# Reordering the Hyena transforms of a two-block transformer kernel: wide products on VectorE, GpSimd without arithmetic there, tables loaded early, gate projections between the steps

## The reference, cut to what matters

```python
def long_conv_bidir(u, h_fwd, h_bwd, bias):
    k2 = jnp.concatenate([h_fwd, jnp.zeros((1, C)), h_bwd[:0:-1]], axis=0)
    U = jnp.fft.rfft(u, n=2 * L, axis=1)
    K = jnp.fft.rfft(k2, n=2 * L, axis=0)
    y = jnp.fft.irfft(U * K[None], n=2 * L, axis=1)[:, :L]
    return y + u * bias

def hyena_mixer(hv, hx1, hx2, ...):
    z, gates = parts[0], parts[1:]          # after a short convolution
    for n in range(2):
        z = gates[n] * long_conv_bidir(z, filt[:, 0, n], filt[:, 1, n], bias[n])
    return z

m = sigmoid(g_na) * (y_na @ w_na_o) + sigmoid(g_hy) * (y_hy @ w_hy_o)
x = x + g1 * (m @ w_out)                    # then the feed-forward part, then a norm
```

## Time and profile before

| | us |
|---|---|
| median of three runs | 1063.85 |
| lowest, highest | 1062.31, 1063.89 |
| profiled execution, device time | 1062.26 |
| its span in the profile | 1060.4 |
| PE busy | 997.3 (94%) |
| DVE (VectorE) busy | 830.4 (78%) |
| ACT (ScalarE) busy | 566.2 (53%) |
| POOL (GpSimd) busy | 166.7 (16%) |

### The profile page before, as it was taken

One profiled execution on the slowest core, in us unless ns is written; L12 is line 12 of the kernel. 1 busy time (PEld: TensorE's weight loads), 2 busy tenths in 40 slices (PEclk: granted clock), 3 DMA queues, 4 the chain that ended last, 5 costly groups with the idle time before them and its releaser, 6 DMA issues.

```text
span 1060.4 us, 19534 instructions
## 1 busy us (share of the span) xinstructions
PE 997.3 (94%) x7946; PEld 964.0 (91%) x7946; DVE 830.4 (78%) x1360; ACT 566.2 (53%) x1062; POOL 166.7 (16%) x172
## 2 busy tenths in 40 slices
PE   7798999999899999999999999998798999999996
PEld 7798999999898879999999988988798899999996
DVE  7799999686898876899977678888888667776453
ACT  7544444435676655555555535665354456665442
POOL 5113222101000003001201110221632210000001
PEclk9899999999999999999999999999999999999998
DMA  9546466665434323788856613331334435645441
GB/s 289 210 162 227 168 240 210 228 226 212 174 124 153 127 100 135 275 335 304 289 213 238 224 53 143 120 135 60 160 120 159 160 131 189 214 184 192 167 159 40
DMA packets 33721, 192.19 MB, mean 181 GB/s; under 512 B 4912, under 2 KB 6256, under 8 KB 14816
## 3 DMA queue, kind: packets, MB, share of 16 engines
q1 hardware_dynamic: 23520, 157.46, 40.7%
q10 hardware_dynamic: 6912, 25.17, 7.0%
q0 software_dynamic: 3200, 8.32, 2.5%
HBM read 187.78 MB, written 3.15 MB: 180 GB/s over the span
## 4 chain that ended last, share of the span: by engine, by line
PE 66%; DVE 21%; ACT 6%; issue 3%; DMA 2%; POOL 1%; DVEq 0%; SPq 0%; ACTq 0%
PE ps L93 64%; DVE wl L70 7%; ACT wh L67 3%; DVE ab L70 3%; DMA raw<-w 2%; PE ps L96 1%; DVE junk L84 1%; DVE s L77 1%; DVE fh L70 1%; ACT s L67 1%; POOL wl L70 1%; DVE hl L70 1%; DMA cst<-cst 1%; DVE s L84 0%; DVE x L73 0%
## 5 line engine op out<-in xcount | busy, mean ns | idle before, releaser
L70 DVE TENSOR_TENSOR wl<-raw,wh 128x1024 fp32r<-128x1024 f32 x276 | 340.4, 1248 | 39.1 <-ACT wh L67 38.8
L67 ACT ACTIVATE wh<-raw 128x1024 fp32r<-128x1024 f32 x286 | 294.9, 1049 | 8.1 <-DMA raw<-w 3.4
L93 PE MATMUL ps<-xh,wh 128*128 128x256 f32 (+1 forms) x992 | 280.6, 283 | 5.9 <-ACT sghy L67 2.5
L93 PE MATMUL ps<-xh,wl 128*128 128x256 f32 (+1 forms) x992 | 278.3, 281 | 0.0
L93 PE MATMUL ps<-xl,wh 128*128 128x256 f32 x992 | 278.1, 280 | 0.0
L93 PE MATMUL ps<-xt,wh 128*128 128x272 f32 (+1 forms) x1120 | 224.9, 295 | 12.7 <-DVE fg L70 5.9
L93 PEld LDWEIGHTS ps<-xt,wh 128*128 128x128 f32 x1120 | 181.9, 193 | 17.6 <-DVE fg L70 7.0
L93 PEld LDWEIGHTS ps<-xh,wh 128*128 128x128 f32 x992 | 188.6, 190 | 7.1 <-ACT sghy L67 2.7
L93 PEld LDWEIGHTS ps<-xh,wl 128*128 128x128 f32 x992 | 189.1, 191 | 0.2
L93 PEld LDWEIGHTS ps<-xl,wh 128*128 128x128 f32 x992 | 188.7, 190 | 0.0
L93 PE MATMUL ps<-xt,wl 128*128 128x272 f32 (+1 forms) x560 | 162.5, 290 | 0.0
(11 more groups left out here) (333 smaller groups left out, 1665.2 us busy)
## 6 DMA issues: line engine op xcount, KB each, us to landing
raw<-w SPq DMA_DIRECT2D x141, 1024.0 KB, 4.9
ada<-ada ACTq DMA_DIRECT2D x37, 512.0 KB, 4.4
cb<-ada ACTq DMA_DIRECT2D x11, 512.0 KB, 3.4
raw<-w SPq DMA_DIRECT2D x4, 512.0 KB, 6.4
spare<-w SPq DMA_DIRECT2D x2, 1024.0 KB, 9.5
spectra<-ev POOLq DMA_DIRECT2D x8, 256.0 KB, 3.6
ks<-spectra POOLq DMA_DIRECT2D x2, 1024.0 KB, 6.2
skew<-rpb POOLq DMA_DIRECT2D x8, 192.0 KB, 3.2
```

Of the source, the lines that this page charges most:

```text
L67: return Issued(self.e and self.e.activation(out, src, func, **kw))
L70: return Issued(self.e and self.e.tensor_tensor(out, a, b, op))
L93: return Issued(self.e and self.e.matmul(out, stat, mov, start=start, stop=stop))
```

## The change

The transforms are written anew around the same arithmetic.

1. `fwd_dve`, `fwd_pool` and `fwd_end_dve` become `fwd_split`, `fwd_products`, `fwd_sums` and `fwd_low`, all on VectorE. The four products of a half are two instructions of 128x1024 in place of four of 128x512, two of which were GpSimd's.
2. GpSimd makes no low parts of gate halves any more. It issues DMAs, and does no arithmetic between the last score bias and the sums `m` of the merge (six of the eight, VectorE does the last two).
3. The table F is loaded before the attention and split there; G and half of the first spectrum (`ksh`) are loaded before the attention ends.
4. The transforms (0,0) and (0,1) begin inside the attention's last steps. The other steps stand at new places between the gates. All forward transforms use banks 3 and 4, all inverse ones 5 and 6, all transposes 7.
5. Slot 5 comes back into the ring for the fourth half of the output projection and no longer for its first.

```diff
     def on_pool(self, h):
-        g = self.W.half_of(("gate", 0))
-        return h < 3 or (g <= h < g + 16 and (h - g) % 3 == 2)
+        return h < 3
...
             if h == last:
-                order.insert(0, 5)
+                order.insert(3, 5)
...
     (second_pe)
-        self.na_turn(P, 3, 1, 0), self.na_turn(P, 3, 1, 1)
+        self.na_turn(P, 3, 1, 0)
+        self.fwd_pe(P, 0, 0)
+        self.na_turn(P, 3, 1, 1)
         self.gate_pe(P, 1)
+        self.fwd_pe(P, 0, 1)
         self.na_av(P, 7)
...
+    def fwd_products(self, V, n, half):
+        a, b = [self.pair(t) for t in self.fwd_bufs(n, half)]
+        k = self.spectrum(n, half)
...
+        V.tt(b, a, k, ALU.mult).then_inc(S["hy_v"], ("v1", n, half))
+        V.wait_ge(S["hy_v"], ("v1", n, half))
+        V.tt(a, a, k[:, :, ::-1, :], ALU.mult).then_inc(S["hy_v"], ("v2", n, half))
+    def fwd_sums(self, V, n, half):
...
+        V.tt(b[:, :, 0, :], b[:, :, 0, :], b[:, :, 1, :], ALU.subtract).then_inc(S["hy_v"], ("y1", n, half))
+        V.wait_ge(S["hy_v"], ("v2", n, half))
+        V.wait_ge(S["hy_v"], ("y1", n, half))
+        V.tt(b[:, :, 1, :], a[:, :, 0, :], a[:, :, 1, :], ALU.add).then_inc(S["hy_v"], ("y2", n, half))
+        V.wait_ge(S["hy_v"], ("y2", n, half))
+        V.tt(at[:, :512], bt[:, :512], bt[:, 512:], ALU.add).then_inc(S["hy_v"], ("w", n, half, 0))
+        V.tt(at[:, 512:], bt[:, :512], bt[:, 512:], ALU.subtract).then_inc(S["hy_v"], ("w", n, half, 1))
...
     def tail_pe(self, P):
-        gate(2)
-        self.fwd_pe(P, 0, 0)
-        gate(3)
-        self.fwd_pe(P, 0, 1)
-        gate(4, 5, 6)
+        gate(2, 3, 4)
         self.inv_pe(P, 0, 0)
-        gate(7, 8)
+        gate(5, 6)
+        self.inv_pe(P, 0, 1)
+        gate(7)
         self.fwd_pe(P, 1, 0)
-        self.inv_pe(P, 0, 1)
-        gate(9, 10)
+        gate(8)
         self.fwd_pe(P, 1, 1)
-        gate(11)
+        gate(9, 10, 11)
         self.inv_pe(P, 1, 0)
         gate(12)
         self.hy_back(P, 0)
-        gate(13, 14, 15)
-        self.nao_pe(P, 0), self.nao_pe(P, 1)
+        gate(13, 14)
         self.inv_pe(P, 1, 1)
-        self.nao_pe(P, 2), self.nao_pe(P, 3)
+        gate(15)
         self.hy_back(P, 1)
-        for d in range(4, 8):
+        for d in range(8):
             self.nao_pe(P, d)
...
     (second_pool: early loads)
+        for m in (0, 1):
+            G.dma(self.ksh[:, 512 * m:512 * (m + 1)]..., self.kd[0, ...]).then_inc(S["ld_ksh"], ...)
+        G.dma(self.dftg[:, :], self.ins["dft1"][:, 512:1024]).then_inc(S["ld_dftg"], ("load",), by=16)
```

More of the change, by code:

```diff
@@ L417, in cast, with casts @@
         A.act(self.wh[s][:, :], src, ACT.Copy).then_inc(self.S["w_hi"], use)
-    def casts(self, A, spent):
+    def casts(self, A, spent, most=None):
         W = self.W
-        while A.next_half < W.halves:
+        end = W.halves if most is None else min(W.halves, A.next_half + most)
+        while A.next_half < end:
             b = W.before[("half", A.next_half)]
@@ L440, in rests @@
         V.spent = max(V.spent, spent)
-        while V.next_half < W.halves:
+        end = W.halves if most is None else min(W.halves, V.next_half + most)
+        while V.next_half < end:
             b = W.before[("half", V.next_half)]
@@ L2071, in second_act @@
             ath(2 * p, 0), ath(2 * p, 1)
-            soft(4 * p + 3)
+            if p < 3:
+                soft(4 * p + 3)
         self.z_hi(A, 0, 0), self.z_hi(A, 0, 1)
+        soft(15)
         self.gate_act(A, 0)
         oh(6)
+        self.fwd_act(A, 0, 0)
+        A.wait_ge(S["ld_dftg"], ("load",))
+        A.wait_ge(S["na_v"], ("min", 15))
+        A.act(self.GH[:, :], self.dftg[:, :], ACT.Copy).then_inc(S["hy_a"], ("tab", 1))
         ath(7, 0), ath(7, 1)
         self.gate_act(A, 1)
+        self.fwd_act(A, 0, 1)
         oh(7)
@@ L2261, in second_pool @@
                     S[f"ld_skew{hd % 2}"], ("head", hd + 2), by=16)
+        for m in (0, 1):
+            G.wait_ge(S[f"st_kd{m}"], ("kd", 1, 1))
+        G.wait_ge(S["na_v"], ("min", 14))
+        for m in (0, 1):
+            G.dma(self.ksh[:, 512 * m:512 * (m + 1)].rearrange("p (i c) -> p i c", i=2),
+                  self.kd[0, :, 1024 * m:1024 * (m + 1)].rearrange("p (i c) -> p i c", i=2)[:, :, 0:256]).then_inc(
+                S["ld_ksh"], *([("load",)] if m else []), by=16)
         G.wait_ge(S["proj"], self.W.freed5)
[L2263 removed]
+        G.dma(self.dftg[:, :], self.ins["dft1"][:, 512:1024]).then_inc(S["ld_dftg"], ("load",), by=16)
     def gate_pe(self, P, i):
@@ L2365, in fwd_dve @@
-        V.wait_ge(S[f"ld_ks{n}"], ("load",))
-        for m, (a, b) in enumerate(((a0, b0), (a1, b1))):
-            V.wait_ge(S["hy_v"], (f"u{m}", n, half))
-            V.tt(self.two(b), self.two(a), self.spectrum(n, half, m), ALU.mult).then_inc(
-                S["hy_v"], ("v1", n, half, m))
-        for m, b in enumerate((b0, b1)):
-            V.wait_ge(S["hy_v"], ("v1", n, half, m))
-            V.tt(b[:, :256], b[:, :256], b[:, 256:], ALU.subtract).then_inc(S["hy_v"], ("y1", n, half, m))
@@ L2399, in fwd_end_dve, with fwd_low @@
+    def fwd_low(self, V, n, half):
+        S, a = self.S, self.fwd_bufs(n, half)[0]
+        yh, yl = self.YS[half]
+        for par in (0, 1):
             s = slice(512 * par, 512 * (par + 1))
```

269 lines of the change are left out of this document (133 added, 136 removed).

## The result

The changed kernel takes 1044.75 us in the median (four runs, 1044.12 to 1050.02); the kernel before, beside it, 1063.57 (four runs, 1062.31 to 1063.89). The ratio is 0.9836, with a 95% interval of 0.9803 to 0.9869: 14 to 21 us faster. The profiled execution took 1044.12 us with a span of 1042.3, 18.1 us less than the profiled one before.

A forecast was written before the change was run, and what follows sets the result against it. It took TensorE, 94% busy and waiting in the stage mostly for VectorE, as the bound: 20.6 us of waits and clock, less 6.0 new waits, plus 1.8, gives 16.4 us less, forecast 1047, range 1041 to 1054.

The forecast's parts named there:

- Two-engine blocking: In the stage, VectorE and GpSimd block each other when both read the buffers; GpSimd's help costs VectorE over 13 us.
- part 3: Five gate-half low parts move to VectorE: +5.8 us, against -2.0 for four halves and -4.6 for two blocked instructions.
- A half of VectorE, 1.2 for a wide product: Transform arithmetic: a 1024-column product takes 1.2 us, a half 8.0 us, 0.5 less than before, all on VectorE.
- slower: Rival, 3%: wide products reading the swapped spectrum run at 5.8 us instead of 1.2, giving 1084.
- The 14.8 us of waits and 5.8 of clock: TensorE's losses from 727.86 to 822.79 us, 20.6 us together, all taken to go, before new waits.
- The new waits, 6.0 us: Walking both engines through their new orders gives TensorE 6.0 us of new waits in the stage, none over 1.4.
- nearly everything goes: Rival, 15%: neighbouring VectorE instructions overlap, so new waits are about 3 us: 1044, or 1042 with the weight wait.
- The output projection, 1.8: In the output projection, three low parts come earlier, two stay in the row, and 1.8 us of `ml` waits go.
- Loads: GpSimd's queue of spectrum and table loads: only table G has no slack, and 0.5 us is allowed.
- loads give back: Rival, 4%: the shorter stage asks for its 1 MB weight loads faster, bounding the gain; near 1060.
- VectorE stays the bound: Rival, 17%: each half takes 1.5 us longer than 8.0, and one 1.7 us clock drop returns: 1053.6.
- No clock loss from small waits: In the stage, new waits of at most 1.4 us bring no low clock; bounds 0 and 5.8 us.

The follow-up runs named there:

- e3: The kernel before, but VectorE instead of GpSimd makes the five low parts of gate halves; 1055.47 us, ratio 0.9927.
- e5: The kernel before with its old order and narrow instructions, but all of the stage's arithmetic on VectorE, none on GpSimd; 1050.78 us, ratio 0.9883.
- e2: The changed kernel, but GpSimd again makes the low parts of gate halves 2, 5, 8, 11 and 14; 1047.38 us, ratio 0.9854.
- e7: The changed kernel plus 40 unused additions of 128x256 on GpSimd, which read two buffers, behind its last spectrum load; 1058.83 us, ratio 0.9955.
- e4: The changed kernel with a half's products as four instructions of 128x512 instead of two of 128x1024; 1045.36 us, ratio 0.9845.
- e1: The changed kernel, but slot 5 comes back for the first half of the output projection, as in the kernel before; 1045.27 us, ratio 0.984.
- e6: The changed kernel, but transforms (0,0) and (0,1) start only after the last attention product, as before; 1046.76 us, ratio 0.9844.
- e8: The changed kernel plus 80 unused memsets on GpSimd, which only write, behind its last spectrum load; 1044.33 us, ratio 0.9845.
- e9: The changed kernel, but VectorE makes low parts of weights (and of x) one step later in Hyena output and output projections; 1041.49 and 1042.03 us.

## Why the prediction was right, and where not

The sign, the size and the cause came out: two engines that blocked each other, a chain on VectorE that made TensorE wait, and a clock that fell behind the waits. That the number came out so close (1047 against 1044.75) is partly luck: the new waits alone were 4.4 us too large, and other errors made up for a part of it. Its steps one by one:

**Two-engine blocking.** The step said that GpSimd's help cost VectorE over 13 us. e3 and e5 show 10.7 us of the stage from taking GpSimd's arithmetic away, e2 4.8 from the other side, and e7 that blocking alone does it. Right, and it is the main part of the gain. The price on VectorE was even higher than the step said: the table's low parts took 3.25 us a pair for 1.29, and `zl`, the weights' low parts and the sums were stretched too. From cut to cut VectorE's busy time fell by 8.8 us (87.91 to 79.08), where the terms of part 3 (+5.8, -2.0, -4.6) give 0.8.

**A half of VectorE, 1.2 for a wide product.** Measured 1.22, and sums, subtractions and low parts at 0.69, or 1.29 to 1.42 a pair. The rival *slower*, a wide product at 5.8, is out. But a half is not faster because of the width (e4).

**The 14.8 us of waits and 5.8 of clock.** All went: clock 1.00, no wait over 0.9. The stretch is 94.93 - 76.88 = 18.05 us shorter; 20.6 less the 1.64 that came would be 19.0. The 0.9 between lies in the clock term: TensorE's busy time fell by 4.8 us (79.78 to 74.95), not by 5.8. A part of that is a slower pace of the changed kernel's matmuls at clock 1.00 (next step).

**The new waits, 6.0 us.** This is the mis-sized term: in the stretch they measured 1.64. One by one, forecast and measured:

| wait | forecast | measured |
|---|---|---|
| transposes of tiles 12 and 13 | 1.2 + 0.2 | 0.29 |
| attention product on `natl` | 0.5 | none |
| first forward transform | 0.85 | none |
| last attention product on `natl` | 0.4 | none |
| inverse (0,1) on `yl` | 1.4 | 0.88 |
| gate 14 on its low part | 1.4 | 0.47 |

TensorE in the changed kernel, the three that are left:
```profile
728.35 1.36 PE L96 MATMUL ps<-cst,s 128*128 128x128 f32 x8 [0.29 <-DVE s L77]
...
758.75 0.39 PE L93 MATMUL ps<-yh,gh 128*128 128x256 f32 x1 [0.88 <-DVE yl L70]
...
785.10 0.39 PE L93 MATMUL ps<-xh,wh 128*128 128x256 f32 x1 [0.47 <-DVE wl L70]
```
The walk moved VectorE by 0.7 us for the low part of half 2 and left TensorE where it was. In fact both came later, VectorE by 0.4 us (its `s` 13.13 us behind the cut, 12.74 before), TensorE also by 0.4 before the stretch begins (715.79 to 727.86 is 12.07 us before, 714.68 to 727.19 is 12.51 after), so the gap that opened between them was small. Only a part of TensorE's delay comes from `natl`, which it waited for behind that low part. The rest is chance: in this execution its matmuls ran at a slower pace, at a granted clock of 1.00. TensorE in the changed kernel, the first and the last of the 24 matmuls of one projection:
```profile
724.37 0.28 PE L93 MATMUL ps<-xh,wh 128*128 128x256 f32 x1
...
727.08 0.28 PE L93 MATMUL ps<-xl,wh 128*128 128x256 f32 x1
```
That is 0.118 us a matmul, where the earlier trace rows have 0.114. In the third execution, which ran this part at the faster pace, the wait for `s` was 0.51 us in place of 0.29. The later terms counted every VectorE instruction whole; a pair of 512 columns takes 1.29 us, not 1.38. That was the argument of the rival *nearly everything goes*, whose waits of 3 us and whose 1044 lie nearer to the trace (1.64 and 1044.75) than my walk. The forecast's number held because other terms went the other way: the waits came out 4.4 us smaller than forecast, the clock term 0.9 smaller and the output projection 1.0 smaller, and 1.4 us came back at the end.

**The output projection, 1.8.** It gave 0.8 (36.14 to 35.36). The waits for `ml` fell from 1.8 to 0.5 us and one of 0.54 for a weight's low part went, but a wait of 1.13 us came that I had not looked for:
```profile
814.82 0.39 PE L93 MATMUL ps<-hyh,wh 128*128 128x256 f32 x1 [1.13 <-DVE a L73]
...
821.80 0.39 PE L93 MATMUL ps<-mh,wh 128*128 128x256 f32 x1 [0.51 <-DVE ml L70]
```
VectorE is late for the tile that empties a bank, because ahead of it a low part waits for ScalarE's cast. Undone alone (e1), the term is worth 0.6 us of waits, or 2.4 with the low clock that this execution of e1 had: the 1.8 us were a mis-sized term too.

**The end and the beginning.** 1.4 us came back behind the last `out`, which is no work of the change (below), and 1.1 went ahead of the first cut, within the 9 us by which that cut varies; there the profiled execution before had a stretch at a low clock (0.69 from 665 to 670 us) and the one after none. The whole: -1.1 - 17.6 - 0.8 + 1.4 = -18.1, against -16.4 forecast.

**Loads.** `ksh`, issued at 730.8 and 731.6, landed after 3.6 us in the median and was used at 741.6. The table G, issued at 732.3, landed after 3.7, in time for its cast at 737.2. Tile `dftg`:
```profile
DMA to landing us min/median/max: 3.7/3.7/3.7
```
No releaser among TensorE's waits is a load; the rivals *loads give back* and *VectorE stays the bound* are out. The Trainium skill ("SBUF — State Buffer", "Who interferes with whom") has it that DMAs issued by GpSimd can starve while VectorE is in a two-port mode; no run here shows it.

**No clock loss from small waits.** Right for the three executions of the changed kernel (1.00 throughout the stage), but that no wait up to 1.9 us had been followed by a low clock before was no rule to build on: in e1 none of the waits was over 1.30 us, and 0.57 followed (above). e1 agrees with the rule of the Trainium skill that I had set against it ("TensorE: Matmul & The Clock Gate", there "A second HAM failure mode: psum-queue depth-cycling"), that frequent short idles can bring the low clock back. The changed kernel does not test it, since little was left of the cluster of small waits.

**What gave what.** By the stretch to the last `nao`, in the order before, e3, e5, e6, after: low parts off GpSimd 5.9 us, products and sums off GpSimd 4.8, tables, gates, banks and width 2.4, the early start 4.4. These are differences of single executions, with their low clocks and paces in them. Another order of the steps may share it out otherwise: the low parts are worth 5.9 from before and 4.8 from after.

## What to carry to other kernels

Before work is shared out to GpSimd, compare the durations of VectorE's instructions that lie under GpSimd's with the same forms elsewhere in the trace: help that reads SBUF can cost more than it saves. Cut the two profiles at the same instructions before you subtract totals, since here the start of one and the same instruction varied by 9 us, while the changed kernel's stage agreed within 0.2. When you forecast a new wait, move both engines by the work you add, and check whether the waiting one is held up by it too. Before you call a difference of 1 or 2 us the worth of an edit, look whether a low clock lies in it.

## What the runs showed of the hardware that I had not expected

**Blocking by reads alone.** e7 and e8 above. Beside 256-column additions on GpSimd an instruction of 1024 columns grew from 1.22 to 1.66 us and one of 512 from 0.69 to 1.17, some 0.5 us more each. Beside a low part of 2.4 us on GpSimd an instruction cost 1.1 us more (1.22 to 2.33), 1.8 (0.49 to 2.28) or, a pair, 2.9 (1.29 to 4.14). Beside the same kind of GpSimd instruction, VectorE's short and long instructions lost about the same in e7; beside the longer one all lost more.

**The clock behind a wait.** Stretches of e3, e5 and e2 that follow waits of 5.3, 2.7 and 3.4 us for `yl`, and of e6 behind its wait of 2.2:
```profile
760.39:768.00 7.61, 7.61 (x46) 7.61 (x47) 6.39 (x9) 5.42 (x10) 0.00 (x0) 0.67 0.37 139
```
```profile
758.68:764.00 5.32, 5.32 (x34) 5.32 (x35) 4.87 (x6) 3.33 (x7) 0.00 (x0) 0.71 0.53 165
```
```profile
762.00:768.00 6.00, 6.00 (x41) 6.00 (x41) 4.99 (x5) 2.87 (x6) 2.38 (x1) 0.72 0.38 158
```
```profile
754.00:760.00 6.00, 5.87 (x51) 5.87 (x52) 5.69 (x8) 0.50 (x1) 0.00 (x0) 1.00 0.01 3
```
TensorE was busy throughout the first three, so their means cost 2.5 us (7.61 at 0.67), 1.5 and 1.7. So part of what a wait costs stands behind it: of the 4.8 us of e2, 1.0 (TensorE's busy time from cut to cut, 87.04 to 88.08) to 1.7 are clock. Length alone does not decide: before, a wait of 2.3 was followed by a drop and one of 2.5 was not (1.00 from 804 to 810 us), and in e1 a drop stood behind 1.30 and 0.52.

**Two pitches of the same loop.** In the last feed-forward loop some executions advance by 7.77 us for each output tile and others by 7.48, at a granted clock of 1.00 in both; first the changed kernel, then the same kernel in its third run:
```profile
1000.49 0.48 DVE L73 SCALAR_TENSOR_TENSOR x<-ps,mod,x 128x256 f32<-128x256 f32 x1 [2.36 <-PE ps L93]
1008.26 0.48 DVE L73 SCALAR_TENSOR_TENSOR x<-ps,mod,x 128x256 f32<-128x256 f32 x1 [2.36 <-PE ps L93]
```
```profile
999.82 0.48 DVE L73 SCALAR_TENSOR_TENSOR x<-ps,mod,x 128x256 f32<-128x256 f32 x1 [2.06 <-PE ps L93]
1007.30 0.48 DVE L73 SCALAR_TENSOR_TENSOR x<-ps,mod,x 128x256 f32<-128x256 f32 x1 [2.06 <-PE ps L93]
```
The same two paces, 0.118 and 0.114 us a matmul, show in parts of the stage. Of the fourteen profiled executions five had the slower pitch in the last loop (two of the changed kernel, e2, e4 and e5) and nine the faster (before and the third of the changed kernel among them). With it the stretch to the end is 0.7 to 1.4 us longer (table above, 202.5 to 203.2 against 201.8 to 201.9, e9 left out). In the stretch to the last `out` the second execution of the changed kernel and e4 ran at the slower pace, at 36.0 us against 35.35. It belongs to the execution, not to the program: the third execution of the changed kernel had the faster pitch. What sets it stays open. What was expected of the two runs that repeated the changed kernel; the first had its median in the range (1045.85), but its runs spread from 1041.23 to 1049.06; the second came out below its range, at 1042.44:

> The changed kernel again, on the same chip as the three others, as their measure. One of its four runs was 1050.02 at an unchanged clock. Expected 1044 to 1046 in most runs; if the 1050 comes back in one of five, the kernel has a second mode, and the profiles show whether the matmul pitch of a stage differs.

> The changed kernel a third time, beside the variant. It showed 5.72 and 7.77 in both profiles. Program: 5.72 and 7.77 again. Execution: either pair. Time 1044 to 1047.
